# A 2048-wide transformer stack in float32 on one core: the low parts of the weights written over the raw weights, eight places for the high parts, and a loader that waits for TensorE

## The reference

```python
h = h + 0.5 * swiglu(rmsnorm(h, ffn1_norm), ffn1_w_in, ffn1_w_out)      # 2048 -> 2*5632 -> 2048
u = rmsnorm(h, mix_norm) @ w_in_mix                                      # pooling + gated linear attention
h = h + concat([y_pool, y_gla]) @ w_out_mix
h = h + 0.5 * swiglu(rmsnorm(h, ffn2_norm), ffn2_w_in, ffn2_w_out)
x = rmsnorm(h, final_norm)
x = layer_norm(ALPHA * x + mixer_a(x)); x = x + (p0 @ w_ple0) * sigmoid(x @ w_gate0)   # indexed sparse attention
x = layer_norm(ALPHA * x + mixer_b(x)); x = x + (p1 @ w_ple1) * sigmoid(x @ w_gate1)   # stick-breaking attention
```

## Time and profile before

| | |
|---|---|
| three runs, median | 2707.23 us |
| the profiled execution | 2708.06 us |
| its span | 2706.3 us |
| TensorE (PE) busy | 2693.3 us, 12182 matmuls |
| VectorE (DVE) busy | 1565.3 us |
| ScalarE (ACT) busy | 1304.3 us |
| DMA moved | 550.06 MB, mean 203 GB/s |
| mean granted TensorE clock | 1.00 |

### The profile page before, as it was taken

The page is one execution under the profiler, slowest core; times in us unless marked ns, Lnnn a source line. Parts: engine busy times, 40 slices in busy tenths (PEclk is TensorE's granted clock), DMA queues, the critical chain, the costliest instruction groups (busy, mean ns, idle before and its releaser), DMA issues.

```text
span 2706.3 us, 34354 instructions
## 1 busy us (share of the span) xinstructions
PE 2693.3 (100%) x12182; PEld 2221.6 (82%) x12182; DVE 1565.3 (58%) x1946; ACT 1304.3 (48%) x1728; POOL 57.6 (2%) x63
## 2 busy tenths in 40 slices
PE   8999999999999999999999999999999999999999
PEld 7888888888888788888888888887888888878887
DVE  6555555555734466555555555668556586567566
ACT  6443444344544455443444444555554464575463
POOL 0000000000000000000000000030000000021000
PEclk9999999999999999999999999999999999999999
DMA  9876677676745467776676666764457576546754
GB/s 307 260 217 194 208 215 217 194 213 200 251 154 162 146 224 222 219 217 202 201 221 213 199 208 202 233 212 157 147 177 253 163 223 226 176 140 203 238 181 137
DMA packets 422136, 550.06 MB, mean 203 GB/s; under 512 B 40976, under 2 KB 267536, under 8 KB 421232
## 3 DMA queue, kind: packets, MB, share of 16 engines
q1 hardware_dynamic: 420352, 539.90, 64.0%
q0 software_dynamic: 1504, 8.34, 0.9%
q10 hardware_dynamic: 144, 0.04, 0.0%
HBM read 525.06 MB, written 23.07 MB: 203 GB/s over the span
## 4 chain that ended last, share of the span: by engine, by line
PE 98%; SPq 1%; DMA 0%; ACT 0%; DVE 0%; issue 0%; ACTq 0%; DVEq 0%
PE bank L1366 31%; PE bank L1368 31%; PE bank L1367 31%; PE bank L1325 1%; PE bank L1076 0%; PE bank L832 0%; PE bank L816 0%; DMA raw<-in_ffn_w_in_dram 0%; PE bank L1067 0%; SPq L1244 0%; PE bank L1060 0%; PE bank L516 0%; PE bank L786 0%; PE bank L528 0%; PE bank L823 0%
## 5 line engine op out<-in xcount | busy, mean ns | idle before, releaser
L1710 DVE TENSOR_TENSOR wlo<-raw,whi 128x1024 fp32r<-128x1024 f32 (+2 forms) x975 | 1151.7, 1186 | 1081.3 <-ACT whi L1451 1076.1
L1451 ACT CAST whi<-raw 128x1024 fp32r<-128x1024 f32 (+2 forms) x975 | 987.8, 1018 | 1283.3 <-PE bank L1368 1272.0
L1366 PE MATMUL bank<-whi,p_hi 128*128 128x512 f32 x2016 | 790.7, 392 | 4.9 <-DVE wlo L1710 4.0
L1368 PE MATMUL bank<-whi,p_lo 128*128 128x512 f32 x2016 | 784.8, 389 | 0.0
L1367 PE MATMUL bank<-wlo,p_hi 128*128 128x512 f32 x2016 | 784.6, 389 | 0.0
L1366 PE MATMUL bank<-whi,q_hi 128*128 128x512 f32 x1696 | 664.3, 392 | 0.5 <-DVE wlo L1710 0.5
L1368 PE MATMUL bank<-whi,q_lo 128*128 128x512 f32 x1696 | 660.3, 389 | 0.0
L1367 PE MATMUL bank<-wlo,q_hi 128*128 128x512 f32 x1696 | 660.1, 389 | 0.0
L1366 PEld LDWEIGHTS bank<-whi,p_hi 128*128 128x128 f32 x2016 | 378.6, 188 | 87.7 <-issue 9.3
L1368 PEld LDWEIGHTS bank<-whi,p_lo 128*128 128x128 f32 x2016 | 378.5, 188 | 79.0
L1367 PEld LDWEIGHTS bank<-wlo,p_hi 128*128 128x128 f32 x2016 | 378.7, 188 | 78.6 <-issue 1.2
(11 more groups left out here) (288 smaller groups left out, 1006.5 us busy)
## 6 DMA issues: line engine op xcount, KB each, us to landing
raw<-in_ffn_w_in_dram SPq DMA_DIRECT2D x704, 256.0 KB, 3.0
raw<-in_ffn_w_out_dram SPq DMA_DIRECT2D x320, 256.0 KB, 3.3
raw<-in_w_in_a_dram SPq DMA_DIRECT2D x192, 256.0 KB, 3.1
raw<-in_w_in_mix_dram SPq DMA_DIRECT2D x128, 256.0 KB, 3.2
raw<-in_w_ple_gate_dram SPq DMA_DIRECT2D x128, 256.0 KB, 3.8
raw<-in_w_in_b_dram SPq DMA_DIRECT2D x128, 256.0 KB, 3.1
raw<-in_w_out_mix_dram SPq DMA_DIRECT2D x64, 256.0 KB, 3.4
raw<-in_w_o_a_dram SPq DMA_DIRECT2D x64, 256.0 KB, 3.8
```

The lines of the kernel that those rows point to most:

```text
L1366: pe.matmul(o, xht, wh, start=(kt == t_first), stop=False)
L1368: ins = pe.matmul(o, xlt, wh, start=False, stop=(kt == t_last))
L1451: act.copy(whi[:, c % SPLIT, 0:n, 0:w], raw[:, c, 0:n, 0:w]).then_inc(hi_done, 1)
L1710: dve.tensor_tensor(wlo[:, c % SPLIT, 0:n, 0:w], raw[:, c, 0:n, 0:w], whi[:, c % SPLIT, 0:n, 0:w].bitcast(F32), ALU.subtract).then_inc(lo_ ...
```

## The change

`wlo` becomes an overlay of `raw`: both are eight chunks at the same addresses, and VectorE writes the low part of a chunk over its raw weights. `whi` grows from four places to eight, so that the sum of the buffers is as before (64 KB on each partition). The preset of `chunk_used`, `USED0`, goes from 4 to 8: ScalarE may split a chunk when TensorE is done with the one 8 before it. Since the low part now lies where the next weights land, the loader waits for `chunk_used` in place of `lo_done`: chunk g is loaded when TensorE has used chunk g-8. One more wait keeps the first row sums of squares behind the warm-up matmuls. The special order of the last round keeps its constant under the name `LAST`.

```diff
-SPLIT = 4
+LAST = 4
...
-        raw = sb("raw", [P, CH, 2, NB])
-        whi = sb("whi", [P, SPLIT, 2, NB], F32R)
-        wlo = sb("wlo", [P, SPLIT, 2, NB], F32R)
+        aw = overlaid([("raw", [P, CH, 2, NB], F32)], [("wlo", [P, CH, 2, NB], F32R)])
+        raw, wlo = aw["raw"], aw["wlo"]
+        whi = sb("whi", [P, CH, 2, NB], F32R)
...
-        LO0, USED0, FREE0, HID0 = CH, SPLIT, 2, 2
+        LO0, USED0, FREE0, HID0 = CH, CH, 2, 2
...
-                        sp.wait_ge(lo_done, (s.r0 + k) * CH + (c + 1))
+                        sp.wait_ge(chunk_used, (s.r0 + k) * CH + (c + 1))
...
-                        wh, wl = whi[:, c % SPLIT, j, 0:s.width], wlo[:, c % SPLIT, j, 0:s.width]
+                        wh, wl = whi[:, c, j, 0:s.width], wlo[:, c, j, 0:s.width]
...
             for n in range(WARM):
-                pe.matmul(bank[3][:, 0:SEQ], sgw[:, 0, 0:P], sgw[:, 1, 0:SEQ], start=True, stop=True)
+                ins = pe.matmul(bank[3][:, 0:SEQ], sgw[:, 0, 0:P], sgw[:, 1, 0:SEQ], start=True, stop=True)
+            ins.then_inc(sem("warmed"), 1)
...
-                act.copy(whi[:, c % SPLIT, 0:n, 0:w], raw[:, c, 0:n, 0:w]).then_inc(hi_done, 1)
+                act.copy(whi[:, c, 0:n, 0:w], raw[:, c, 0:n, 0:w]).then_inc(hi_done, 1)
...
             def x_squares(blk):
 
+                act.wait_ge(sem("warmed"), 1)
...
-                dve.tensor_tensor(wlo[:, c % SPLIT, 0:n, 0:w], raw[:, c, 0:n, 0:w], whi[:, c % SPLIT, 0:n, 0:w].bitcast(F32),
+                dve.tensor_tensor(wlo[:, c, 0:n, 0:w], raw[:, c, 0:n, 0:w], whi[:, c, 0:n, 0:w].bitcast(F32),
                                   ALU.subtract).then_inc(lo_done, 1)
```

More of the change, by code:

```diff
@@ L1415, in round_ @@
                                 pe.wait_ge(t_done, s.need[c])
-                        if s is last and k == s.n - 1 and c >= SPLIT:
-                            if c == SPLIT:
+                        if s is last and k == s.n - 1 and c >= LAST:
+                            if c == LAST:
                                 for t in range(TT):
-                                    for c_ in range(SPLIT, CH):
+                                    for c_ in range(LAST, CH):
                                         ins = multiply(s, k, u, c_, dst, tiles[0], tiles[-1], (t,))
```

## The result

The change makes the kernel slower, by more than forecast:

| | us |
|---|---|
| kernel before, median of 4 runs | 2707.33 (2707.22 to 2708.42) |
| kernel after, median of 4 runs | 2803.82 (2798.22 to 2814.96) |
| ratio | 1.0363, 95% interval 1.0351 to 1.0375 |
| forecast | 2765, range 2730 to 2797 |
| the profiled execution of after | 2814.96, its span 2813.3, mean granted clock 0.991 |

The account below looks back on a forecast made before the run. TensorE was taken as the bound, busy 2693.3 of 2706.3 us. Terms 29.5 + 2.8 + 8.4 + 12.5 + 3 + 1.2 = 57.4 us gave 2765 us, range 2730 to 2797.

Parts of the forecast that it names:

- loop term: `ffn_in` loop rounds: TensorE stands 0.95 us at the next round's start, in 31 rounds, 29.5 us.
- residual term: Residual blocks: nothing lost behind 16 tiles, 0.6 us each for six behind 12 tiles, 3 us.
- rival C: Clock falls behind the two 6 us waits, 2.7 to 5.4 us each, giving 2770 to 2776; chance 0.12.
- Earlier splits: ScalarE running up to 8 chunks ahead: taken as 0 us, bounds -4.5 and 0.
- U: The moment in an `ffn_in` round when TensorE finishes chunk 3; next round's first matmul due at U+10.7.
- Blocks 6 and 7: Last squares blocks of the four 8-round stages: 0.7 and 2.1 us each, 2.8 and 8.4 us.
- Block 5: Last squares block of the two 6-round stages, needed by chunk 6: 6.2 us each, 12.5 us.
- Narrow stages: Next stage's first chunk, loaded when the first narrow chunk is used: 0.6 us late, twice, 1.2 us.
- A: Store and move together 1 us shorter, so the loop rounds cost nothing: 25 us, 2732; chance 0.14.
- B: Transfers collide more, store and move losing 0.9 us more between them: 37 us more, 2802; chance 0.15.
- D: Not slower: squares go out early enough and earlier splits take away 4.5 us of waits, 2703; chance 0.05.
- The move: Squares' 256 KB move: 4.1 us to landing, the measured median, kept against 2.6 us from the Trainium skill.

Follow-up runs that it names:

- Experiment 1: Kernel before, with only the loader's wait changed to TensorE's use of the chunk eight before; four places and own memory kept: 2810.04 us.
- experiments 2: Kernel after, with the squares' store and move behind the loads of chunks 1 and 2 instead of 3 and 4: 2731.83 us.
- Experiment 6: Kernel after, with the split of moved squares put behind the splits of the next round's first weights on ScalarE and VectorE: 2757.43 us.
- experiment 4: Kernel after, with the squares' move directly behind their stores, ahead of the load of chunk 4: 2764.01 us.
- Experiment 3: Kernel after, with stores and moves of both squares and residual blocks behind the loads of chunks 1 and 2: 2726.42 us.
- experiment 7: Kernel after, with extra unread identity matmuls ahead of TensorE's wait for the last block of squares in the first `ffn_out` rounds: 2791.88 us.
- experiment 5: Kernel after, with the squares' store and move one chunk later, behind the loads of chunks 4 and 5: 2986.14 us.

## Why the prediction was right in direction and short in size

**In short.** The direction and the mechanism came out as forecast: the loader's later wait makes the squares late, and TensorE pays once a round. What failed is the sum. Its loop term took 3.1 us from the first store to the move, from a single row, where 3.55 was the mean. Its residual term took the landing of a calmer stretch, 3.4 to 5.0 us, where 6.3 was measured. And the clock's fall, which rival C names, was put at nothing in it, where the profiled execution lost 19 us. The paragraphs below take the terms in order.

**What bounds the kernel, and the mechanism: right.** TensorE had no slack to give, and SP's 1417.3 us of waiting in the earlier trace rows were slack that the squares' stores and moves lived on. Experiment 1 shows that the loader's wait alone makes the loss; experiments 2 and 6 cut the chain at its two ends, and each brings the loops' 44.0 us to nothing.

**Earlier splits, 0: right.** Experiment 1 has no more places than before and is as slow as after. With the loops' loss removed, what could be credited to the places is 0.7 to 1.6 us in 44 rounds (experiments 2 and 6).

**The loop, 29.5 forecast, 44.0 measured.** Each step, from the 32 blocks in these rounds:

| | forecast | mean measured |
|---|---|---|
| stores start | U+1.25 | U+1.29 |
| first store to move | 3.1 | 3.55 |
| move to landing | 4.1 | 3.98 |
| landed to first chunk split | 3.1 | 3.05 |
| first chunk split | U+11.6 | U+11.87 |

The failed step is the term "from their start to the move's are 3.1 us". I took it from one round, and that round was among the shortest: over the same 32 blocks the kernel before already took 3.10 us or more for this step. Without the first four, which stand at the program's start, its mean was 3.29, and after's is 3.53. So of the 0.44 that I had too little nearly 0.2 was in the choice of one row, and some 0.24 came with the change. In the earlier trace rows the stores have a little air behind the loads, and after the change they are issued directly behind them. That the transfers of chunk 3 hold them up fits experiment 4, where chunk 4's load is out of the way and the step is as long, but wasn't tested by itself. The restart, which I had left out, costs 0.1 more: the first step between matmuls is 0.34 instead of 0.23. Ready 1.17 late and 0.11 of restart are 1.28 of the 1.33 us that a round lost (44.0 less one fall of the clock early in the program, over 32). The term was a small difference of large ones, 11.6 less 10.7, so 0.4 more on the way made it almost half as large again: 31 x 0.4 is 12 of the 14.5 us missing here. My bounds for it, 0 and 53, did hold.

**Blocks 6 and 7, 11.2 forecast, 21.5 measured.** The four first rounds lost 6.01, 6.01, 3.35 and 6.12 us; 2.8 (0.7 + 2.1) was forecast for each. Both parts were short. Before the first chunk the rounds lost 1.08, 1.80, 0.87 and 0.45. Before chunk 7 TensorE stood 3.36, 2.74, 2.32 and 3.07 us beyond its step, against 2.1: from the first store to the move of block 7 were 3.9 to 4.5 us, where I had 3.3. These waits are 15.7 of the 21.5. Nearly all of the rest, 5.8, is the clock behind three of the waits before chunk 7; the round of 3.35 is the one without a fall. The restarts of the second and the third round:

```profile
493.20 0.50 PE L1366 MATMUL bank<-whi,q_hi 128*128 128x512 f32 x1 [2.58 <-DVE q_lo L1753]
...
1301.10 0.50 PE L1366 MATMUL bank<-whi,p_hi 128*128 128x512 f32 x1 [2.16 <-DVE p_lo L1753]
```

The stretches behind these two restarts, with the granted clock as the third number from the end:

```profile
494.50:500.00 5.50, 5.50 (x19) 4.35 (x18) 5.50 (x7) 4.50 (x5) 0.00 (x0) 0.69 0.21 58
1301.20:1306.00 4.80, 4.80 (x21) 3.94 (x22) 4.77 (x5) 4.80 (x6) 0.00 (x0) 1.00 0.26 91
```

The first stretch lost 0.31 of 5.5 us, which is 1.7. It looks as if the length of the wait decided. But other runs don't bear that out. Experiment 6 has a longer wait at such a place, with no fall behind it:

```profile
207.42 0.50 PE L1366 MATMUL bank<-whi,q_hi 128*128 128x512 f32 x1 [3.23 <-DVE q_lo L1753]
```

```profile
207.40:213.00 5.60, 5.58 (x25) 4.62 (x26) 2.53 (x4) 2.38 (x3) 0.00 (x0) 1.00 0.33 98
```

Experiment 1 has a shorter one in a loop round, with a fall:

```profile
1410.27 0.50 PE L1367 MATMUL bank<-whi,q_hi 128*128 128x512 f32 x1 [1.79 <-DVE wlo L1711]
```

```profile
1410.20:1415.00 4.80, 4.73 (x14) 3.74 (x15) 4.77 (x8) 2.42 (x5) 0.00 (x0) 0.64 0.33 113
```

So waits of 2 to 3 us end with a fall or without one, and what decides it stays open here.

**Block 5, 12.5 forecast, 18.8 measured.** The two rounds lost 10.37 and 8.47. The waits before chunk 6 were 7.14 and 6.60 us beyond the step, against 6.2 each, and the first chunks were 0.62 and 0.17 late. The clock took the rest: it stood at 0.50 for 6.1 us behind the first wait (3.0 us lost, some of them in the next round) and for 3.4 us behind the second (1.7). Nearly right but for the clock.

**Residual blocks, 3 forecast, 16.0 measured.** This step failed outright. SP's queue behind `ffn1_out2`, on the way into `mix_pool`, shows it:

```profile
772.56 3.03 SPq L1211 DMA_DIRECT2D block_squares<-hidq  x4
...
777.73 0.33 SPq L1217 DMA_DIRECT2D hidf<-block_squares  x1
778.10 5.85 SPq L1244 DMA_DIRECT2D raw<-in_w_in_mix_dram  x10
```

The same move among the issues of that microsecond, with KB and us to landing:

```profile
hidf<-block_squares SPq DMA_DIRECT2D x1, 512.0 KB, 6.3
```

I had stores to move at 4.0 and the landing at 3.4 to 5.0. Here they are 5.2 and 6.3, because the block moves among ten weight loads that are issued around it. ScalarE got it at 784.04, TensorE waited for what followed, and ran at half clock behind it (2.7 us of the place's 16.0, and 1.7 more in `a_index`):

```profile
789.22 1.09 PE L1325 MATMUL bank<-con,h 128*128 128x128 f32 x8 [1.28 <-DVE h L1819]
...
792.88 0.77 PE L1366 MATMUL bank<-whi,p_hi 128*128 128x512 f32 x1 [2.56 <-DVE wlo L1712]
```

Experiment 3, which sends these blocks earlier, halves the place. I priced a transfer by the median of a calmer stretch, though the change itself moves the block into a busier one.

**Narrow stages, 1.2 forecast, 6.4 measured.** 3.1 and 3.3 us in place of 0.6 each. In `mix_qk` I priced the load of the first chunk at 3.0 to land; it took 3.7, after a later issue, and TensorE began at 835.89 behind a wait, again with the clock falling (1.7 of the 3.1). In `a_kv` the load landed in 3.0 and no fall followed. 0.9 us was lost there at the first chunk, and 1.4 and 1.0 behind waits for ScalarE's `ikt` (1.17) and GpSimd's `ikd` (1.05), which are work beside the weights that the forecast didn't have. No experiment touched this place; it is at 3.9 to 6.6 in all of them.

**The rivals.** A (the chain just fits, 2732) fell with the loops' 1.33 us a round. B (collisions, 2802) names the time that was measured, which is luck: its 0.9 us in store and move is seen at a third (0.45 more from store to move, 0.12 less to land), and the rest of its sum isn't where it put it. C (the clock) was the right mechanism and too small: I had it behind the two 6 us waits only, at 2.7 to 5.4 each. The profiled run shows 3.0 and 1.7 us for these, and seven more falls behind waits of 1.9 to 3.2 us. The page that I had cited for it, the Trainium skill ("TensorE: Matmul & The Clock Gate", "What's actually happening"), has the clock fall to 1.2 GHz after idling; the trace agrees, with matmuls of 0.43 us a step against 0.23, and in experiment 7 matmuls without any use kept it up at the six places. D fell: nothing passed the wait ahead of U.

**The move: the row held.** I had 4.1 us to landing from the row, and after's median is 3.9. The 2.6 us that I set against it come from a fit that the Trainium skill ("DMA: Bandwidth & Descriptors", "Anatomy of one DMA") gives for transfers issued by GpSimd; these moves are issued by SyncE, so that section states no price for them. In experiment 4, with no load issued directly ahead, the move took 2.7, near that figure. That this is what a transfer costs that meets no other isn't shown, since other loads were still under way.

**What was missing in the range.** The loops' 14.5 us and the clock's 25 us at most would each have fitted; with the residual blocks' 13 and the 5 of the narrow stages they didn't. I had added each rival to the forecast alone, though B and C don't exclude each other, and terms that all come from "later and more crowded" err in the same direction.

## What to carry to other kernels

Before a wait of an issuing queue is made later, list everything that is issued behind it, and measure each of those against its own due time; a wait that costs its own user nothing can hold back someone else's store or move. Issue the small transfers with a due time first, ahead of the loads that have slack, and put the consumer's split of late data behind the work that TensorE needs next: either alone won back the loops' whole loss. Where waits of TensorE of about 2 us or more are forecast, count the clock as a possible loss behind each: 1.5 to 3.1 us here where it fell. Where a term is a small difference of large ones, read each step from many rounds and not from one.

## What the runs showed of the hardware that I had not expected

- TensorE's clock fell from 1.00 to 0.50 behind single waits in a stream that was otherwise full. It fell behind a wait of 1.79 us in experiment 1 and not behind one of 3.23 in experiment 6; behind the loops' usual 0.75 in after it didn't. The price was 1.5 us a fall in the loops of experiment 5, and 1.6 to 3.1 in after's first rounds of `ffn_out`. One kernel's runs differ by it: 2798.22 at a mean clock of 0.996, 2814.96 at 0.991.
- Matmuls of 128 columns whose results nobody reads (56 in 6.41 us at a 12-tile wait) held the clock at 1.00 through the waits before the last block. The kernel won 12 us by the medians, and 10.6 in these six rounds by the profiles.
- One 256 KB move took 3.9 us (median of 44) with 512 KB of loads issued directly ahead of it, and 2.7 with none.
- A move of 512 KB among ten weight loads took 6.3 us to land, where the nine moves of residual blocks in that run have a median of 3.8.
